# Norm factors as two columns, 512-column matmuls in the last stage, and a join of three units, in a two-block kernel

## The reference

```python
a = modulate(rmsnorm(h, norm1_g), shift1, scale1)          # and the same for the context
q, k, v, r = split(a @ w_in)                               # 4 heads of 128 (q, k) and 256 (v, r)
log_a = log_sigmoid((a @ w_a1[d]) @ w_a2[d] + b_a[d]) / 16 # per direction d
o = bidirectional gated linear attention, 4 heads, from the context's final state
h = h + gate1 * ((head_rmsnorm(o) * silu(r)) @ w_o)
h = h + gate2 * (relu(modulate(rmsnorm(h, norm2_g)) @ w1) ** 2 @ w2)   # inner width 4096
return rmsnorm(h, final_g)
```

## Time and profile before

| | |
|---|---|
| three runs | 982.64, 984.57, 988.10 us (median 984.57) |
| the profiled execution | 987.62 us, its span 985.8 us |
| TensorE busy | 951.1 us of the span (96%), 7434 matmul instructions |
| VectorE busy | 797.0 us (81%), 371.3 of them L1325 (306 of 1220 ns) |
| ScalarE busy | 556.4 us (56%), 321.1 of them L839 (306 of 1053 ns) |
| DMA | 197.28 MB, 200 GB/s in the mean |
| mean granted clock of TensorE | 0.993 |
| dense matmuls of the last stage | 883.4 to 975.5 us |

### The profile page before, as it was taken

One profiled execution on the slowest core, in us unless ns is written; L12 is line 12 of the kernel. 1 busy time (PEld: TensorE's weight loads), 2 busy tenths in 40 slices (PEclk: granted clock), 3 DMA queues, 4 the chain that ended last, 5 costly groups with the idle time before them and its releaser, 6 DMA issues.

```text
span 985.8 us, 21262 instructions
## 1 busy us (share of the span) xinstructions
PE 951.1 (96%) x7434; PEld 922.3 (94%) x7434; DVE 797.0 (81%) x1301; ACT 556.4 (56%) x893; POOL 1.2 (0%) x6
## 2 busy tenths in 40 slices
PE   8999999999999999999999999999999799999996
PEld 7999999999999899999999998878898799999996
DVE  6998899998989689999998888757568777776443
ACT  7445666665546656666655656885422465664432
POOL 0000000000000000000000000000000000000000
PEclk9999999999999999999999999999999989999998
DMA  8776575556886464555555884653761447766651
GB/s 316 266 257 222 167 257 182 186 189 195 259 268 230 162 213 150 179 192 184 185 177 180 290 274 165 221 173 128 257 214 65 158 142 233 225 228 217 192 166 43
DMA packets 53878, 197.28 MB, mean 200 GB/s; under 512 B 5982, under 2 KB 6110, under 8 KB 53696
## 3 DMA queue, kind: packets, MB, share of 16 engines
q1 hardware_dynamic: 53680, 195.49, 59.7%
q10 hardware_dynamic: 144, 1.05, 0.3%
HBM read 195.46 MB, written 1.05 MB: 199 GB/s over the span
## 4 chain that ended last, share of the span: by engine, by line
PE 80%; DVE 11%; ACT 4%; DMA 3%; issue 2%; DVEq 0%; SPq 0%; ACTq 0%
PE ps L442 22%; PE ps L444 22%; PE ps L443 22%; DVE wlo L1325 4%; DMA raw<-stream 2%; ACT whi L839 2%; PE ps L472 1%; PE ps L473 1%; PE ps L474 1%; PE ps L488 1%; DVE rstd L1352 1%; PE ps L536 1%; PE ps L538 1%; PE ps L537 1%; PE ps L682 1%
## 5 line engine op out<-in xcount | busy, mean ns | idle before, releaser
L1325 DVE TENSOR_TENSOR wlo<-raw,whi 128x1024 fp32r<-128x1024 f32 x306 | 371.3, 1220 | 84.9 <-ACT whi L839 84.2
L839 ACT ACTIVATE whi<-raw 128x1024 fp32r<-128x1024 f32 x306 | 321.1, 1053 | 101.5 <-DMA raw<-stream 55.8
L442 PE MATMUL ps<-xhi,whi 128*128 128x256 f32 x1288 | 365.0, 283 | 4.8 <-ACT cval L1151 1.8
L444 PE MATMUL ps<-xhi,wlo 128*128 128x256 f32 x1288 | 362.0, 281 | 0.0
L443 PE MATMUL ps<-xlo,whi 128*128 128x256 f32 x1288 | 362.0, 281 | 0.0
L442 PEld LDWEIGHTS ps<-xhi,whi 128*128 128x128 f32 x1288 | 243.7, 189 | 6.9 <-issue 3.4
L443 PEld LDWEIGHTS ps<-xlo,whi 128*128 128x128 f32 x1288 | 243.7, 189 | 0.7 <-issue 0.5
L444 PEld LDWEIGHTS ps<-xhi,wlo 128*128 128x128 f32 x1288 | 243.6, 189 | 0.0
L442 PE MATMUL ps<-yhi,whi 128*128 128x256 f32 x400 | 112.8, 282 | 3.1 <-DVE wlo L1325 3.1
L443 PE MATMUL ps<-ylo,whi 128*128 128x256 f32 x400 | 112.3, 281 | 0.0
L444 PE MATMUL ps<-yhi,wlo 128*128 128x256 f32 x400 | 112.3, 281 | 0.0
(11 more groups left out here) (288 smaller groups left out, 1442.1 us busy)
## 6 DMA issues: line engine op xcount, KB each, us to landing
raw<-stream SPq DMA_DIRECT2D x362, 512.0 KB, 3.8
h<-xT SPq DMA_DIRECT2D x2, 512.0 KB, 5.1
c<-ctxT ACTq DMA_DIRECT2D x1, 1024.0 KB, 6.8
ct<-cst SPq DMA_DIRECT2D x1, 962.5 KB, 10.3
rt_tab<-rot SPq DMA_DIRECT2D x1, 896.0 KB
cr<-crow SPq DMA_DIRECT2D x1, 512.0 KB, 7.1
state<-crow SPq DMA_DIRECT2D x1, 512.0 KB, 8.1
out<-h SPq DMA_DIRECT2D x1, 512.0 KB, 2.6
```

The costliest lines, as they stand in the source:

```text
L442: pe.matmul(dst, whi[:, w], at(hi, k), start=(k == 0), stop=False)
L444: last = pe.matmul(dst, wlo[:, w], at(hi, k), start=False, stop=(k == K - 1))
L839: c.sig(act.activation(whi[:, s * D:(s + 1) * D], raw[:, r * D:(r + 1) * D], ACT.Copy), hi_ready)
L1325: c.sig(dve.tensor_tensor(wlo[:, w], raw[:, r], whi[:, w], ALU.subtract), slots_done)
```

## The change

- The last stage's `mhi` and `mlo` become the two halves of one buffer `m2`. `units` with `both=m2` multiplies `whi` with the matching 256 columns of both halves in one matmul of 512 columns, into the bank's two halves; hi x wlo stays a matmul of 256 columns into the first. VectorE adds both halves to `h`, one after the other.
- For the third and the last norm the stat is two columns: `column_stat_of` holds 128 x 128 of the squares and streams one column of ones, so tokens stand on partitions. Root and reciprocal are of 128 x 2. `spread` turns them back into 128 x 256 in STAT: a factor's column, repeated 128 times as weights, times the identity. The products read the factor from there (`RSTD`). The eighth square of the third norm is no longer added to `ssum`; it is a second matmul operand, as it already was in the last norm.
- The join takes three units of `w_o` side by side, two chunks of one unit before the next unit, five units follow whole. `gla_stat(2)` stands ahead of the first chunks, `gla_stat(3)` ahead of the third; `head_product(hd + 1)` stands inside `head_norm(hd)`. `r_out(7)`, one `hi()` and one `lo()` come ahead of the join, so `resid` has one less (`ahead=1`); the `r` unit 7 comes ahead of `gla_values(1)`.
- The first two `r` units rotate over four banks. `ctx_exponents` 0 and 1 come one unit later, the `exponents` one value unit later, ScalarE's and VectorE's programs to match.

The diff, cut to its core (left out: how new arguments are passed on, and unchanged lines; one level of indentation is taken off):

```diff
@@ -280,8 +280,8 @@
     stage = ExitStack()
-    mhi = sb("mhi", MC * T, F32R, stage)
-    mlo = sb("mlo", MC * T, F32R, stage)
+    m2 = sb("m2", 2 * MC * T, F32R, stage)
+    mhi, mlo = m2[:, 0:MC * T], m2[:, MC * T:2 * MC * T]
@@ -334,6 +334,7 @@
     ones, ident = cst_of("ones"), cst_of("ident")
+    COLS, factors, RSTD = STAT[:, 3 * P:3 * P + 2], spare[:, 4:6], STAT[:, 0:T]
@@ -439,8 +440,12 @@
                         pe.wait_ge(y_ready, final - (K - 1 - k))
-                    pe.matmul(dst, whi[:, w], at(hi, k), start=(k == 0), stop=False)
-                    pe.matmul(dst, whi[:, w], at(lo, k), start=False, stop=False)
+                    if both is None:
+                        pe.matmul(dst, whi[:, w], at(hi, k), start=(k == 0), stop=False)
+                        pe.matmul(dst, whi[:, w], at(lo, k), start=False, stop=False)
+                    else:
+                        halves = both[:, :].rearrange("p (s n) -> p s n", s=2)[:, :, k * T:(k + 1) * T]
+                        pe.matmul(ps[t % lag][:, 0:2 * T], whi[:, w], halves, start=(k == 0), stop=False)
@@ -491,6 +496,24 @@
+
+        def column_stat_of(pieces):
+
+            c.n["root_ready"] = c.n.get("stat_ready", 0)
+            c.again(root_ready)
+            for tk in range(2):
+                for k, piece in enumerate(pieces):
+                    last = pe.matmul(COLS[:, tk:tk + 1], piece[:, tk * P:(tk + 1) * P], ones[:, 0:1], start=(k == 0),
+                                     stop=(k == len(pieces) - 1))
+            c.sig(last, stat_ready)
+
+        def spread():
+
+            pe.wait_ge(rstd_ready, c.n["stat_ready"])
+            for tk in range(2):
+                last = pe.matmul(STAT[:, tk * P:(tk + 1) * P], factors[:, tk:tk + 1].to_broadcast([P, P]), ident,
+                                 start=True, stop=True)
+            c.sig(last, ev("spread"))
@@ -697,18 +720,19 @@
         pe.wait_ge(ev("gate_in"), 2)
-        units(1, DC, xhi, xlo)
+        units(2, DC, xhi, xlo)
...
         ctx_exponents(1)
-        units(2, DC, xhi, xlo)
+        units(1, DC, xhi, xlo)
...
-        moving(V_PARTS, xhi, xlo, {1: lambda: gate_logits(1, 1), 4: exponents_of(0, 0), 5: exponents_of(0, 2),
-                                   6: exponents_of(1, 0), 7: exponents_of(1, 2)})
+        moving(V_PARTS, xhi, xlo, {1: lambda: gate_logits(1, 1), 5: exponents_of(0, 0), 6: exponents_of(0, 2),
+                                   7: exponents_of(1, 0)})
+        exponents_of(1, 2)()
@@ -751,31 +775,32 @@
-        pair = []
+        three = []
...
                 pe.wait_ge(tile_read, tile[0])
-                pair.extend(slot_of_next_unit() for _ in range(2))
-            for k in range(first, last):
-                c.take(y_ready)
-                for j, slot in enumerate(pair):
+                three.extend(slot_of_next_unit() for _ in range(3))
+            c.take(y_ready, last - first)
+            for j, slot in enumerate(three):
+                for k in range(first, last):
...
                     done = pe.matmul(dst, wlo[:, w], at(zhi, k), start=False, stop=(k == DC - 1))
-                    if k == DC - 1:
-                        c.sig(done, pe_units)
+                if last == DC:
+                    c.sig(done, pe_units)
             if last == DC:
-                tile[0] += 2
-
-        def r_units(n):
-            units(n, DC, xhi, xlo, lag=2)
-
-        r_units(2)
+                tile[0] += 3
+
+        def r_units(n, lag=2):
+            units(n, DC, xhi, xlo, lag=lag)
+
+        assert tile[0] % RING == 0
+        r_units(2, RING)
@@ -789,27 +814,32 @@
         gla_scores(2)
+        r_units(1)
         gla_values(1)
-        r_units(1)
...
         gla_values(3)
+        gla_stat(2)
         gla_out_chunks(0, 2)
-        gla_stat(2)
+        gla_stat(3)
         gla_out_chunks(2, 4)
-        gla_stat(3)
-        gla_out_chunks(4, DC)
-        units(DC - 2, DC, zhi, zlo)
-        stat()
+        gla_out_chunks(4, 6)
+        gla_out_chunks(6, DC)
+        units(DC - 3, DC, zhi, zlo)
+        c.take(ssum_ready, 7)
+        pe.wait_ge(ev("n2_square"), 1)
+        column_stat_of([ssum[:, 0:T], at(sq, 1)])
+        spread()
...
         c.n["y_ready"] += LATE
-        looped(DC // 2, 8, MC, mhi, mlo, lag=2, final=c.n["y_ready"])
+        looped(DC // 2, 8, MC, mhi, mlo, lag=2, final=c.n["y_ready"], both=m2)
...
         pe.wait_ge(ev("last_square"), 1)
-        stat_of([ssum[:, 0:T], at(sq, 1)])
+        column_stat_of([ssum[:, 0:T], at(sq, 1)])
+        spread()
@@ -852,6 +882,12 @@
+
+        def sqrt_columns(n, eps=EPS):
+            c.n["rstd_ready"] = c.n.get("root_ready", 0)
+            c.again(rstd_ready)
+            c.take(stat_ready)
+            c.sig(act.activation(root[:, 0:2], COLS, ACT.Sqrt, scale=1.0 / n, bias=eps), root_ready)
@@ -909,11 +945,15 @@
                                              scale=vt[:, bass.ds(i * 4 + (VEC[gain][0] + m), 1)]), xhi_ready)
+                    if last_square and m == 3 and i == 1:
+                        act.wait_ge(ssum_ready, c.value(sq_ready, -1))
+                        act.activation(at(sq, 1), at(h, DC - 1), ACT.Square).then_inc(ev(last_square), 1)
+                        continue
...
-            if ahead or beside_ctx:
+            if ahead or beside_ctx or last_square:
@@ -1189,15 +1229,15 @@
             hi()
+        keys(0)
+        hi()
         ctx_decays(0)
-        keys(0)
-        hi()
-        keys(1)
-        hi()
-        ctx_decays(1)
-        for m in range(2, GH):
+        for m in range(1, 3):
...
             hi()
+        ctx_decays(1)
+        keys(3)
+        hi()
@@ -1250,21 +1290,22 @@
         hi()
+        r_out(7)
+        hi()
+        act.activation(spare[:, 0:1], ones[:, 0:1], ACT.Sqrt)
         head_squares(1)
-        r_out(7)
-        act.activation(spare[:, 0:1], ones[:, 0:1], ACT.Sqrt)
...
         head_root()
+        head_hi(1)
         head_squares(3)
-        head_hi(1)
...
         head_hi(3)
-        resid(1, None)
-        sqrt_stat(D)
+        resid(1, None, last_square="n2_square", ahead=1)
+        sqrt_columns(D)
@@ -1351,6 +1392,11 @@
+
+        def reciprocal_columns():
+            c.take(root_ready)
+            c.sig(dve.reciprocal(factors, root[:, 0:2]), rstd_ready)
+            c.take(ev("spread"))
@@ -1525,12 +1571,12 @@
                         finish(m - 1)
-                    if m == 3:
+                    if m == 3 and not (last_square and i == 1):
...
-            if ahead or beside_ctx:
+            if ahead or beside_ctx or last_square:
@@ -1740,12 +1786,12 @@
-        def modulated(src, g0, s0, lo_dst, units_after=()):
+        def modulated(src, g0, s0, lo_dst, units_after=(), factor=rstd[:, :]):
...
                     c.sig(dve.scalar_tensor_tensor(out=at(a32, k), in0=at(src, k), scalar=gmod[:, g0 + k:g0 + k + 1],
-                                                   in1=rstd[:, :], op0=ALU.mult, op1=ALU.mult), a_ready)
+                                                   in1=factor, op0=ALU.mult, op1=ALU.mult), a_ready)
@@ -1833,14 +1879,11 @@
             final_norm(6 + n)
-        lo_and_dots(1)
-        lo_and_dots(1)
+        lo_and_dots(3)
         ctx_keys(0)
-        lo_and_dots(1)
-        lo_and_dots(1)
+        lo_and_dots(2)
         ctx_keys(1)
-        for n in range(4):
-            lo_and_dots(1)
+        lo_and_dots(3)
@@ -1874,6 +1917,8 @@
                 c.sig(dve.tensor_tensor(at(rsil, k), at(rsil, k), rstd[:, :], ALU.mult), y_f32)
+            if hd + 1 < GH:
+                head_product(hd + 1)
@@ -1890,21 +1935,20 @@
         lo_and_dots(1)
+        lo()
         gla_mask(3)
-        head_product(1)
...
             head_norm(hd)
-            if hd + 2 < GH:
-                head_product(hd + 2)
...
         mod_of(2 * DC, 5 * DC, 1, 4 * DC, "g_n2")
-        resid(1, None, gate=2 * DC)
-        reciprocal_root(rstd)
-        modulated(h, DC, 3 * DC, xlo)
+        clear_sum()
+        resid(1, None, gate=2 * DC, ahead=1, last_square=True)
+        reciprocal_columns()
+        modulated(h, DC, 3 * DC, xlo, factor=RSTD)
@@ -1931,22 +1975,26 @@
                 hm = at(h, first + m)
-                c.sig(dve.scalar_tensor_tensor(out=hm, in0=ps[m][:, 0:T],
-                                               scalar=mod[:, 5 * DC + first + m:5 * DC + first + m + 1]
-                                               if isinstance(first, int) else mod[:, bass.ds(first + (5 * DC + m), 1)],
-                                               in1=hm, op0=ALU.mult, op1=ALU.add), tile_read)
+                for half in range(2):
+                    ins = dve.scalar_tensor_tensor(out=hm, in0=ps[m][:, half * T:(half + 1) * T],
+                                                   scalar=mod[:, 5 * DC + first + m:5 * DC + first + m + 1]
+                                                   if isinstance(first, int) else mod[:, bass.ds(first + (5 * DC + m), 1)],
```

(10 more changed lines are left out.)

14 lines of the change are left out of this document (7 added, 7 removed).

## The result

The changed kernel takes 979.98 us (median of eight runs, 978.82 to 981.40); the kernel before, beside it, 987.01 us (eight runs, 982.64 to 991.08, the three of the prediction among them). The ratio is 0.9925, 95% interval 0.9908 to 0.9942: faster by 7.0 us. Forecast were 976.5 us and a gain of 8.0.

What follows compares the result with a forecast made beforehand. TensorE, working through 96% of the span, was taken as the bound. -1.3 - 2.8 - 1.5 - 1.9 + 0.5 - 1.0 = -8.0 us: 987.62 profiled becomes 979.6, or 976.5 against the median 984.57; range 972.5 to 981.5.

Steps and rivals of the forecast that it cites:

- Taking 3.05 off the profiled execution's time: Base: the profiled 987.62 us was 3.05 above the three-run median 984.57, so 979.6 became 976.5.
- rival (d): Two terms fall short together, merge with join or with dearer columns: 980.3 us, no difference to be told; chance 0.10.
- 1. Gates and values: 620 to 700 us: waits at gate sums and on `cval` go, r units start 1.3 us earlier; bounds 0.8 to 1.8.
- with a restart saved: Gate sums' waits go, so context value units could begin 2.3 us earlier, but VectorE's `decayed` blocks prevent using it.
- 2. Join: Gated attention's output, 749 to 783 us: three units side by side fill TensorE's waits, -2.8 us; bounds -0.9 to -3.1.
- Rival (c): Join only trades waits: VectorE's chain ends no sooner, fifth unit stalls; gains 0.9, 978.4 us; chance 0.12.
- 3. Third norm: 784 to 790 us: column stat, short root and reciprocal, and spread bring the first product 1.5 us earlier; bounds 0.8 to 1.7.
- rival (a): Clock stays up across the third norm's shorter gap: up to 2.0 us sooner, 974.5 us; chance 0.12.
- 4 and 5. Merge and second read-out: Last stage: 512-column matmuls gain 1.9 us (bounds 0 to 3.1); a second product per output lengthens one wait by 0.5.
- (b): Merging in the last stage gains nothing, two pieces being read like two matmuls: 978.4 us; chance 0.14.
- (e): Slower: last-stage 512-column matmuls pause between their distant halves in each of 256 blocks; at 50 ns, 991 us; chance 0.04.
- 6. The end: Last norm, product to output product: columns shorten 4.43 us to 3.4, gain 1.0 with the second product; bounds 0 and 1.2.

Runs made afterwards that it cites:

- experiment 1: The changed kernel with four low parts instead of two between VectorE's two decayed blocks; 977.40 us, ratio 0.9891.
- experiment 9: The changed kernel with four low parts between the decayed blocks and the exact wait count in the last stage; 975.27 us, ratio 0.9878.
- experiment 10: The changed kernel with four low parts, the exact last-stage wait, and unused matmuls filling the third norm's gap; 972.20 us, ratio 0.9853.
- experiment 12: The kernel before once more, nothing edited; 989.24 us (one run).
- experiment 4: The kernel before with only the last stage's 512-column matmuls and their second read-out; 986.46 us, ratio 0.999.
- experiment 6: The changed kernel with TensorE's last-stage wait asking for the exact position in each turn; 978.62 us, ratio 0.992.
- experiment 11: The changed kernel once more, nothing edited; 980.86 us, ratio 0.9931.

## Why the prediction was right, and where its sum was off

**The result and the base.** 8.0 us were forecast and 7.0 measured. Of the 3.5 us between 976.5 and 979.98, 2.4 lie in the base: 984.57 was the median of three runs, that of eight is 987.01. Taking 3.05 off the profiled execution's time was the larger error. The measured 979.98 is above the 979.6 under which the prediction would call it faster, and nearer to rival (d)'s 980.3 than to the forecast: the time alone could not tell these two apart. It is faster against the base of eight runs, and (d) is out by the stretches, since join and merge each gave about what was forecast.

**1. Gates and values, -1.3, measured +0.06.** The steps held: waits at the exponents gone, TensorE 2.4 us early at the context's values, no use of it because of the `decayed` blocks, `cval` wait gone. The failed step is "with a restart saved": the forecast let the 2.3 us turn into a wait at no further price. The wait of 2.0 us can bring the clock down, which costs 1.65: six traces have this wait, in four the parts behind take 26.64 to 26.70 us (clock 0.50), in two 25.03 and 25.04 (clock 1.00). In these two the whole stretch takes 106.03 and 105.94 us, 1.0 and 1.1 under before, next to the forecast; in the four it takes 107.11 to 108.11. The old order without the `cval` wait takes 105.05 and 105.52, so by these traces the reorder as made is a loss of 0.4 to 3.1 us (the part ahead of the context's values varies by 1 us between executions of one order), and what gained was the banks of the r units. With four low parts between the blocks the reorder pays: 103.99, 103.18 and 103.09 us (experiments 1, 9, 10). The kernel before can pay such a price as well: its wait of 1.78 us on `cval` was followed by a fall in one of three traces, for 1.43 us (experiment 12).

**2. Join, -2.8, measured -2.94**, and -2.88 by itself. Three units in, one wait of 0.61 us left ("about 1"): step and size right. The sum had a slip: three units done at 766.4 in place of two at 766.2, and one unit less behind them, are -2.65; the 0.15 for the mid-join restart lay within those times already. Rival (c) is out.

**3. Third norm, -1.5, measured -1.19.** Too cheap were the column calls (0.22, priced at 0.14) and the spread (0.94 to the product, priced at 0.7); the factor from PSUM did cost nothing (three products in 1.26). For columns at no cost the bound should have been 2.1, not 1.7 (1.5 and four calls of 0.14). The clock was at 0.50 from 784 to 790 us, as kept in the sum, so rival (a) did not come; the price put on it, up to 2.0, was 1.2 to 1.8 when it was taken away. The reason given was thin: the 4.0 us from the end of the dense matmuls to the fall were one execution's figure, and in the twelve traces without filling the fall comes 2.3 to 5.5 us after the last matmul of `w_o` starts. That moves the pair of first units too: from the last matmul of `w_o` to the third unit the old code takes 14.60 us in the trace used here, 15.12 and 15.18 in two others (experiments 4 and 12), the changed kernel 13.41 and 13.42. The gain is 1.2 to 1.8, with the forecast's 1.5 in between.

**4 and 5. Merge and second read-out, -1.9 + 0.5, measured -1.57.** The wait grew by 0.59 (0.85 to 1.44), at the place named. So the merge gives 2.16 in this pair of traces, 8.4 ns a block, and 9.4 or 5.4 ns a block by the pace of the small matmuls that it replaces (experiment 4), all within the bounds 4.2 to 10.5 set by the two 512-column rows. By the Trainium skill's 2.5 ns for each matmul (TensorE: Matmul & The Clock Gate, "Wait — 56ns, not 53.3ns?") it would have been 0.6, an estimate from that page. The traces do not agree: at either pace it is more than twice that, 1.4 or 2.4 us. Rivals (b) and (e) are out. The price of the second read-out was right, its reason was not: what the forecast took for VectorE's way round was a wait for a unit two further on (experiment 6).

**6. The end, -1.0, measured -0.07.** Of the 0.94 us by which the end is longer than the forecast 3.4, two terms hold all: the spread, 1.26 from its start to the product (priced at 0.6 and a hop), and the column calls, 1.12 from the first to the root (priced at 0.7 and a hop). The granted clock is 0.66 from 971 to 972 us and 0.50 in the next, so the spread runs slowly; in the sixth experiment's trace it was 1.00 there, the same spread lasted 0.71, and from the last matmul to the output's product it took 4.16 us instead of 4.68. That trace would be a gain of 0.6, the tenth experiment's, where the clock falls earliest (5.17 us), a loss of 0.4: the forecast had no term for the clock here, and 1.0 came in none.

**Not in the sum:** `mlp_up`, -0.96, with no edit there. It is the pace that this execution drew (experiments 11 and 12); what sets it stays open. Without it the profiled gain would be 6.0, not 6.9: part of the agreement is this stroke of luck.

## What to carry to other kernels

A wait that is taken from the bounding engine moves on to the next place where a helper is late, and if it piles up there into one long wait, the clock can fall, and the slow stretch behind it costs nearly as much again (2.0 and 1.65 us here): look for long blocks of the helper (here 5.5 us twice, two weights apart) and spread them before pulling the bounding engine forward. When a wait's releaser makes no sense as a need, check the awaited count: here a step of nine in place of eight cost 1.6 us. Before a microsecond between two traces is put to an edit, look at a stretch that no edit touches, and at the pace and the clock in both. And compare against a median of many runs of before, or against the profiled execution itself, not a mixture.

## What the runs showed of the hardware that was not expected

Dense 256-column matmuls at a granted clock of 1.00 run at one of a few paces, which hold over long stretches. In `mlp_up` a unit of 24 takes 2.816 us (117.3 ns each) in eight of fourteen traces and 2.848 us (118.7 ns) in six, with nothing between; over 30 units that is 0.96 us. In the first long stretch, which is the same in every kernel, seven traces have 117.3 ns, two 118.7 and five 120.0, which is up to 2.0 us over its 743 matmuls. The pace does not belong to the program: the changed kernel ran that stretch at 117.3 and at 118.7, the kernel before as well, and the kernel before changed its pace within one execution at a wait of 0.85 us and did not in another. That each of the two kernels kept its pace in `mlp_up` need be no more than chance. The other shares of the windows do not tell the paces apart (DMA 0.72 to 0.76 in `mlp_up` in both). What sets it was not found.

After the wait of 2.0 us among the context's values the clock fell to 0.50 in four traces of six, and after the old order's 1.78 us on `cval` in one of three; in the five traces with no wait over 0.5 us there it fell in none. A wait of that length is a risk, then, with a price (1.65 and 1.43 us here) that one execution may show and the next not.
